# The second attention as one shifted sequence of sixteen two-map units

## The reference

```python
z = h @ w_in;  aq, ak, av, bq, bk, bv = split(z)      # h: 256 tokens; the same for 256 context tokens
bq = rms_norm(bq, qn_g);  bk = rms_norm(bk, kn_g)     # group b: per head of 64
aq, ak, bq, bk = apply_rope_2d(...)                   # latent tokens only
# group a: 4 heads of two maps each, values 128 wide
s = einsum('bqhid,bkhid->bhiqk', q, k) * 64 ** -0.5;  p = softmax(s)
o = einsum('bhqk,bkhe->bqhe', p[:, :, 0] - lam * p[:, :, 1], v)
o = rms_norm(o, subln_g) * (1.0 - lam_init)
# group b: 8 query heads on 2 key/value heads
p = softmax(einsum('bqgrd,bkgd->bgrqk', q, k) * 64 ** -0.5)
o = einsum('bgrqk,bkgd->bqgrd', p, v)
y = concatenate([oa, ob]) @ w_out
x = layer_norm(alpha * x + g1 * y)
x = layer_norm(alpha * x + g2 * mlp(modulate(x, sh2, sc2)))
# mod = silu(c) @ ada_w[l] + ada_b[l] gives shifts, scales and gates, six parts of 1024 a layer
```

## Time and profile before

| | us |
|---|---|
| median of 3 runs | 2010.83 |
| lowest and highest | 1999.68, 2014.06 |
| the profiled execution | 2004.5 |
| its span | 2002.6 |
| end of the last projection before the attention (bv) | 1297.3 |
| start of the scores | 1318.5 |
| start of the output projection | 1419.9 |

### The profile page before, as it was taken

How to read it: one execution, slowest core, us unless ns; L and a number is a source line. 1 busy time by engine, 2 the same in 40 slices (tenths; PEclk the granted TensorE clock), 3 DMA queues, 4 the chain that set the end, 5 groups by cost and what they waited for, 6 DMA issues and landing times.

```text
span 2002.6 us, 38381 instructions
## 1 busy us (share of the span) xinstructions
PE 1820.7 (91%) x13930; PEld 1692.1 (84%) x13930; DVE 1279.4 (64%) x2470; ACT 834.3 (42%) x1510; POOL 112.5 (6%) x101
## 2 busy tenths in 40 slices
PE   6989899999999777899999998967889997889997
PEld 5946899999998545799999998845789997879996
DVE  4455468788744898755655564286666666756665
ACT  4433455455454000255555543322344443434443
POOL 0000000000000454200000000000010001010000
PEclk8979899999999899999999998988999998999999
DMA  6445445555566455355555562310235653525552
GB/s 249 148 147 169 129 156 178 184 177 185 176 180 197 180 209 189 136 179 184 203 180 186 179 227 86 103 44 1 85 116 178 187 182 105 165 97 179 180 187 73
DMA packets 86492, 315.07 MB, mean 157 GB/s; under 512 B 9616, under 2 KB 9760, under 8 KB 86048
## 3 DMA queue, kind: packets, MB, share of 16 engines
q1 hardware_dynamic: 75600, 275.28, 42.6%
q10 hardware_dynamic: 10688, 37.95, 5.3%
q0 software_dynamic: 144, 1.05, 0.1%
HBM read 313.19 MB, written 1.05 MB: 157 GB/s over the span
## 4 chain that ended last, share of the span: by engine, by line
PE 83%; DVE 9%; issue 4%; DMA 1%; ACT 1%; POOL 1%; DVEq 0%; ACTq 0%; POOLq 0%; SPq 0%
PE bank L440 14%; PE bank L441 14%; PE bank L442 14%; PE acc L440 10%; PE acc L441 10%; PE acc L442 10%; PE bank L739 2%; PE bank L522 2%; PE acc L500 2%; DVE route L1599 1%; PE acc L850 1%; POOL route L1264 1%; PE acc L495 1%; DVE arena L1614 1%; DVE small L1704 1%
## 5 line engine op out<-in xcount | busy, mean ns | idle before, releaser
L1304 DVE TENSOR_TENSOR w_lo<-raw,w_hi 128x512 fp32r<-128x512 f32 x982 | 652.8, 689 | 474.6 <-ACT w_hi L934 473.6
L934 ACT ACTIVATE w_hi<-raw 128x512 fp32r<-128x512 f32 x982 | 593.8, 628 | 418.8 <-PE acc L440 268.4
L440 PE MATMUL bank<-x_hi,w_hi 128*128 128x256 f32 x2224 | 639.6, 288 | 53.9 <-issue 22.7
L441 PE MATMUL bank<-x_lo,w_hi 128*128 128x256 f32 x2224 | 636.6, 286 | 0.0
L442 PE MATMUL bank<-x_hi,w_lo 128*128 128x256 f32 x2224 | 636.3, 286 | 0.0
L440 PEld LDWEIGHTS bank<-x_hi,w_hi 128*128 128x128 f32 x2224 | 434.7, 195 | 60.0 <-issue 39.2
L441 PEld LDWEIGHTS bank<-x_lo,w_hi 128*128 128x128 f32 x2224 | 434.7, 195 | 0.0
L442 PEld LDWEIGHTS bank<-x_hi,w_lo 128*128 128x128 f32 x2224 | 434.5, 195 | 0.0
L440 PE MATMUL acc<-x_hi,w_hi 128*128 128x256 f32 x1024 | 290.2, 283 | 0.0
L441 PE MATMUL acc<-x_lo,w_hi 128*128 128x256 f32 x1024 | 289.8, 283 | 0.0
L442 PE MATMUL acc<-x_hi,w_lo 128*128 128x256 f32 x1024 | 289.8, 283 | 0.0
(11 more groups left out here) (231 smaller groups left out, 1891.8 us busy)
## 6 DMA issues: line engine op xcount, KB each, us to landing
raw<-in_peer_u SPq DMA_DIRECT2D x128, 512.0 KB, 3.4
raw<-in_peer_v SPq DMA_DIRECT2D x128, 512.0 KB, 3.3
raw<-in_mlp_w SPq DMA_DIRECT2D x128, 512.0 KB, 3.4
ada_x<-in_ada_w ACTq DMA_DIRECT2D x64, 512.0 KB, 3.9
route<-in_ada_w SPq DMA_DIRECT2D x32, 512.0 KB, 4.4
raw<-in_w_in SPq DMA_DIRECT2D x25, 512.0 KB, 4.1
raw<-in_conv_w_in SPq DMA_DIRECT2D x24, 512.0 KB, 3.9
raw<-in_attn_w_in SPq DMA_DIRECT2D x18, 512.0 KB, 3.4
```

Source lines behind the costliest of these rows:

```text
L440: first = mm(dst, a[0], b[0], start=start, stop=False, **kw)
L441: mm(dst, a[0], b[1], start=False, stop=False, **kw)
L934: return nc.scalar.activation(dst, src, f, **kw)
L1304: v.tensor_tensor(w_lo[:, unit(n, half)], raw[:, a:a + HALF], w_hi[:, unit(n, half)].bitcast(F32), ALU.subtract).then_inc(s["lo_done"], 1)
```

## The change

The rotation is cut in two. Group a's eight tiles are rotated while bq is projected: PE has four matmuls between the two pairs of bq, DVE has its products between the low parts of weight tiles. The mean squares of group b move ahead of the projection of bv. Group b's norm factors and its rotation go into the first steps of the attention, in acc banks.

The diff, cut to its core (`UNITS_2` is 16, `OA` is 13; `attention_order` gives each unit two banks `sc`, then `ams` once behind unit 15, and four `obc` at the end; `t_bank` is acc2 or acc3, `rotate` is the cosine product and the sum of L1737 and L1740):

```diff
                     *softmax_order(MOBA_H, "ms", "mt", 1), ("wo1", 4), ("ms2", 1), ("q", 8), ("s", 8),
-                    ("u", 64), ("route", 2), ("g", 64), ("lam", 1), ("aq", 2), ("ak", 4), ("bq", 2), ("bk", 1),
-                    ("bv", 1), ("bms", 1), ("bbc", 4), ("rot2", 7), *softmax_order(8, "as", "at", 2),
-                    *softmax_order(16, "bs", "bt", 1, {AMS: ("ams", 2)}), ("wo2", 4), ("mean0", 1), ("var0", 1),
+                    ("u", 64), ("route", 2), ("g", 64), ("lam", 1), ("aq", 2), ("ak", 4), ("bq0", 1), ("rot2", 4), ("bq1", 1), ("bk", 1), ("bms", 1),
+                    ("bv", 1), *attention_order(), ("wo2", 4), ("mean0", 1), ("var0", 1),
...
+        sm_pt = cut2(2 * 2 * 512)
+        sm_p = arena[:, 0:2 * 2 * 512]
...
-            ada(ada_at + ADA_RING, 2 * N_MOD * KC)
...
             mlp("mlp0", ins["mlp_w1"][0], ins["mlp_w2"][0])
+            sp.wait_ge(s["ada_row_full"], ADA_1 + ADA_GATES + 1)
+            for n in range(ada_at + ADA_RING, ada_at + 2 * ADA_RING):
+                load_ada(n, slot_free=True)
...
-            project_two("bq", "bq", x_split)
+            project_pair("bq", 0, "bq0", 0, x_split)
+            for k in range(2):
+                wait_freed(pe, "aq", k)
+            for k in range(4):
+                wait_freed(pe, "ak", k)
+            pe.wait_ge(s["in_con2"], 16)
+            mean_heads("rot2", C2("rot"), qk, 8 * T)
+            project_pair("bq", 1, "bq1", 0, x_split)
             project_both("bk", 0, "bk", 0)
...
+            def scores(n):
+                if n < 8:
+                    q, tq, k_tiles = n // 2, n % 2, (14 + n // 2, 4 + n // 2)
+                else:
+                    q, tq, k_tiles = 8 + (n - 8) // 2, n % 2, (13, 12)
+                ps = [opened(f"sc{n}_{m}") for m in range(2)]
+                for k, tile in enumerate(k_tiles):
+                    for m in range(2):
+                        r = slice(64 * m, 64 * m + 64)
+                        last = mm(ps[m][:, k * T:(k + 1) * T], qk[r, q * T + tq * P:q * T + (tq + 1) * P],
+                                  qk[r, tile * T:(tile + 1) * T], start=True, stop=True)
+                        if k:
+                            last.then_inc(full(f"sc{n}_{m}"), 1)
...
+            def transposes(n):
+                pe.wait_ge(s["sm2_p"], n + 1)
+                for b in range(1 if n < 8 else 2):
+                    if n in (0, 1):
+                        pe.wait_ge(s["bbc_done"] if n == 0 else s["rotb_done"], 4 if n == 0 else 3)
+                    elif n < 8:
...
+                    a = (n % 2) * 1024 + b * 512
+                    for m in range(4):
+                        last = nc.tensor.transpose(t_bank(n, b)[:, m * P:(m + 1) * P], sm_p[:, a + m * P:a + (m + 1) * P], C("ident"))
+                    last.then_inc(s["tp_full"], 1)
+            def values(n):
+                pe.wait_ge(s["tp_free"], t_count(n, 0 if n < 8 else 1))
+                tq, a = n % 2, (n % 2) * 1024
...
+                tile_q = (n - 8) // 2
+                o = acc[tile_q // 2][:, (tile_q % 2) * T + tq * P:(tile_q % 2) * T + (tq + 1) * P]
                 for kt in range(4):
+                    for g in range(2):
+                        r = slice(64 * g, 64 * g + 64)
+                        p = sm_pt[:, a + g * 512 + kt * P:a + g * 512 + (kt + 1) * P]
+                        last = mm(o[r, :], bv[:, kt * P + 64 * g:kt * P + 64 * g + 64], p, start=(kt == 0), stop=(kt == 3),
+                                  skip_group_check=True)
...
+            pe.wait_ge(s["a_rope"], 1)
+            for i in range(UNITS_2 + 4):
+                if i == 8:
+                    pe.wait_ge(s["b_rope"], 1)
+                if i < UNITS_2:
+                    scores(i)
+                if i == 0:
+                    pe.wait_ge(s["attn_v_ready"], 4)
+                    pe.wait_ge(s["b_rstd"], 1)
...
+                if i == 2:
+                    pe.wait_ge(s["bbc_done"], 4)
+                    for k, n in enumerate((2 * T, 2 * T, T)):
+                        a = 8 * T + 2 * k * T
+                        mm(acc[(0, 1, 3)[k]][:, 0:n], C2("rot"), qk[:, a:a + n], start=True, stop=True).then_inc(s["rotb_full"], 1)
...
+                if 3 <= i < UNITS_2 + 3:
+                    transposes(i - 3)
+                if i >= 4:
+                    if i == 4:
+                        pe.wait_ge(s["rotb_done"], 2)
+                    if i == 12:
+                        wait_freed(pe, "bv")
+                        pe.wait_ge(s["oa_copied"], 2)
+                    last = values(i - 4)
+                    if i - 4 == 7:
+                        last.then_inc(s["attn_oa_full"], 1)
+                if i == OA + 5:
+                    pe.wait_ge(s["oa_mask"], 1)
+                    for g in range(4):
+                        mm(opened("obc", g)[:, 0:T], norm_row("one", g), oa_mask[32 * g:32 * g + 32, :], start=True, stop=True)\
+                            .then_inc(full("obc", g), 1)
...
                 mean(f"mean{n}", res3d, lambda k: wait_res(pe, n, k))
                 mean(f"var{n}", res_sq3d, lambda k: pe.wait_ge(s["ln_sq"], 4 * n + k + 1))
+                if n < ADA_2:
+                    ada(ADA_1 + ADA_GATES + n, acc[0], acc[1], first=True)
+                    ada_columns(ADA_1 + ADA_GATES + n, acc[1])
...
             def mlp(n):
+                pe.wait_ge(s["ada_cols_ready"], ADA_1 + ADA_GATES + n + 1)
                 zero_acc()
...
+            def copies(n):
+                for b in range(1 if n < 8 else 2):
+                    act.wait_ge(s["tp_full"], t_count(n, b))
+                    a = (n % 2) * 1024 + b * 512
+                    fn(sm_pt[:, a:a + 512], t_bank(n, b)[:, :], ACT.Copy).then_inc(s["tp_free"], 1)
+            for i in range(1, UNITS_2 + 4):
+                if i >= 4:
+                    copies(i - 4)
+                if i <= UNITS_2:
+                    exps(i - 1)
+                if i == OA + 1:
                     act.wait_ge(s["oa_ready"], 1)
                     fn(oa_sq, oa_sq, ACT.Square).then_inc(s["oa_sq"], 1)
+                if i == UNITS_2:
+                    wait_full(act, "ams")
+                    fn(oa_std, B("ams")[:, 0:T], ACT.Sqrt, scale=2.0 ** -10, bias=C("eps_small")).then_inc(free("ams"), 1)
+            x_high("mixed2", mixed2, x_hi, 0)
...
+            for k in range(4):
+                wait_full(dve, "rot2", k)
+                turn(qk_rot[:, k * 512:(k + 1) * 512], B("rot2", k)[:, :], 2).then_inc(free("rot2", k), 1)
+                if k % 2:
+                    lo_next("bq", 2 + k // 2)
+            for k in range(4):
+                wait_freed(dve, "rot2", k)
+            step(rotate(0, 4))
+            lo_next("bk", 0)
+            rotate(4, 4).then_inc(s["a_rope"], 1)
+            for name in ("av", "bv"):
                 for q in range(TILE[name][1]):
                     lo_next(name, q)
...
+            def oa_factor():
+                wait_freed(dve, "ams")
+                then_wait(v.reciprocal(oa_mask, oa_std))
                 finite = float(np.sqrt(FMAX / P) / 32.0)
+                v.scalar_tensor_tensor(oa_mask, oa_std, finite, oa_mask, ALU.is_lt, ALU.mult).then_inc(s["oa_mask"], 1)
             def oa_norm():
+                for g in range(4):
+                    a = slice(g * T, (g + 1) * T)
+                    wait_full(dve, "obc", g)
+                    v.scalar_tensor_tensor(mixed2[:, a], B("obc", g)[:, 0:T], lamw[:, 5:6], oa[:, a], ALU.mult, ALU.mult)\
+                        .then_inc(free("obc", g), 1)
+            b_norm(0)
+            b_norm(1)
+            for i in range(1, UNITS_2 + 3):
+                if i == 12:
+                    oa_copy()
+                if i == 13:
+                    oa_clamp()
+                if i <= UNITS_2:
+                    maxima(i - 1)
+                if i == 1:
+                    b_norm(2)
+                    b_norm(3)
+                if 2 <= i <= UNITS_2 + 1:
+                    probabilities(i - 2)
+                if i == 3:
+                    b_turn(0)
+                    b_turn(1)
+                if i == 4:
+                    b_turn(2)
+                    for k in range(3):
+                        dve.wait_ge(s["rotb_done"], k + 1)
+                    rotate(8, 5).then_inc(s["b_rope"], 1)
+                if i == UNITS_2 + 1:
+                    oa_factor()
+            oa_norm()
+            x_low("mixed2", mixed2, x_hi, x_lo, 0)
...
+                if n < ADA_2:
+                    adaln(ADA_1 + ADA_GATES + n, acc[1])
```

More of the change, by code:

```diff
@@ L798, in _ @@
             project_rows("av", [acc[n][:, :] for n in range(4)], tokens, s["attn_v_full"])
+            pe.wait_ge(s["b_sq"], 1)
+            ps = opened("bms")
+            for c in range(6):
+                g = c % 4
+                last = mm(ps[32 * g:32 * g + 32, 0:T], head_means(c // 4), qk_sq[:, c * T:(c + 1) * T], start=(c < 4),
+                          stop=(c >= 2), skip_group_check=True)
```

(15 more changed lines are left out.)

288 lines of the change are left out of this document (107 added, 181 removed).

## The result

The changed kernel took **1952.82 us** (median, 1947.37 to 1955.28), the kernel before beside it 2006.53: ratio 0.9728, 95% interval 0.9682 to 0.9773. So it is faster by 54 us; 42.6 were forecast. The profiled executions took 2004.5 and 1947.37 us, 57 apart.

| stretch | before, us | after, us | difference |
|---|---|---|---|
| start to the first product of aq (code that was not changed) | 1204.72 | 1198.86 | -5.9 |
| from there to the second half of the first `w_out2` tile | 218.98 | 168.76 | -50.2 |
| from there to the end | 578.9 | 578.0 | -0.9 |

A forecast was written before the change was run, and what follows sets the result against it. PE, busy 91% of the span, was taken as the bound. Terms 4.3 + 33.1 + 30.4 + 4 + 7.0 = 78.8 against 126.4, plus 4 clock and 1 norms, gave 42.6 us less: 1968 us, range 1948 to 1988.

The forecast's parts named there:

- the ring through DVE's copy: Group b before: PE's transposes, DVE's copy, PE's products and scores, DVE's maxima form a closed ring, one unit per 3.72 us.
- In front: Ahead of the attention units: four rotation matmuls and the mean squares, moved among the projections, cost PE 4.3 us.
- The cover that I named: Projections of bq, bk and av hide DVE's rotation work of 7.2 us, costed at nothing; uncovered, up to 7.2.
- Group a: First eight attention units, bound by DVE at 2.99 us each, with norm, rotation and other DVE work: 33.1 us.
- Group b and joints: PE's remaining work in group b, 30.4 us with two-head value products at 1.3, plus 4 us for joints between stretches.
- Hand-over: From the last value product to the second half of the output projection's first tile: 7.0 us, 3.2 worse than before.
- Clock: Stops at the start of the unit sequence put PE at the lower level for 8 us, a loss of 4.
- Layer norms: Modulation rounds moved into norms 0 and 1 cost +1 us for both, ends -2 and +5.
- the better end: Rival, chance 0.12: value products fully side by side, no clock fall, norm 0 gets 2 us back: 1959 us.
- The clock's case: Rival, chance 0.10: PE runs at 1.2 GHz through half of the attention sequence: 1984 us.
- projections in the way: Rival, chance 0.10: rotation delays DVE's low parts, PE stands in bq, bk or av up to 7.2 us: 1975.
- the ring: Rival, chance 0.03: the attention ring closes again with one unit in flight, 7.8 us a unit: 2030 us.

The follow-up runs named there:

- run 1: Kernel before, with ScalarE instead of VectorE copying the transposed probabilities out of PSUM: 1992.01 us, ratio to before 0.9936.
- run 2: Changed kernel with the rotation of group a's q and k put back behind the last projection: 1960.68 us.
- run 6: Changed kernel with group b's norm and rotation moved from units 0 to 4 to between the scores of units 7 and 8: 1956.86 us.
- run 3: Changed kernel with the copies of the transposed probabilities put back on VectorE: 1957.85 us.
- run 4: Changed kernel with the value products of a two-head unit of group b issued head after head, not by turns: 1952.61 us.
- run 5: Changed kernel with the scores of a unit issued map after map, not by turns: 1952.03 us.
- run 7: Changed kernel with the two passes that end group b's rotation moved from VectorE to GpSimd: 1953.26 us.
- run 8: Changed kernel with group a's norm broadcasts ahead of the last transposes and group b's output split straight from PSUM: 1942.36 us, ratio to before 0.9696.
- run 9: Changed kernel run again without any edit: 1948.66 us, ratio to before 0.9709.
- run 10: Changed kernel with products of zeros on TensorE as fillers in five of its longest waits: 1948.64 us.
- run 12: Changed kernel with run 8's edit and run 10's fillers except those ahead of w_out2, second execution of that version: 1936.62 us, ratio to before 0.9654.

## Why the prediction was right, and where its sizes were off

The mechanism held: the ring through DVE's copy is shown by run 1, group a bound by DVE and group b by PE by the windows and the timelines. Where the stage's 50.2 us are from: rotation beside the projections 9.3 (run 2), norm beside group a 6.1 (run 6). Run 1 had neither, nor two-head units, and its stage was 205.71, 36.95 above the changed kernel's. Without those two 21.5 are left: two-head units 8 x (5.32 - 3.11) = 17.7, worked out and not run alone, and 3.8 for joints and the rest. With the copy's 13.3 that makes 50.2. In the 3.8 are things that no run moved alone: the modulation rounds, whose matmuls were 4.44 us (L500) and 2.01 us (L495) of PE's busy time inside the stage before, the packed norm, the two groups in one sequence, and against them a hand-over 3.0 us longer (6.8 for 3.8). And the shares depend on the order in which one takes the parts out: the copy is 13.3 in the kernel before (run 1) and 8.2 in the changed one (run 3), and 3.4 of the 9.3 came with the lower level.

Term by term, forecast and measured:

- **In front**: 4.3, and 4.7 (the last projection's work ended 97.30 us from aq, and 92.61 before). The cover that I named held, with no wait of PE inside the projections of bq, bk, av and bv; run 2 shows what it was worth, 5.9 of the 7.2.
- **Group a**: 33.1, and 34.3. DVE as forecast at 3.01 us a unit; until scores and first factors existed it took 2.2 us and not 1.4, and the rest is in small parts.
- **Group b and joints**: 30.4 + 4, and 30.4 together: 26.6 of work and 3.7 of stops (1.24, 0.40, 0.68, 1.37). The work was mis-sized: the value product for two heads was taken at 1.3 us and is 1.02 (-2.2 over eight), and four transposes were taken at 0.6 and are 0.51 when issued in eights (-1.5 over seventeen). For the first the Trainium skill's page "TensorEngine Tiling (Array Packing)", section "Theoretical Speedup", had the better number: its "up to 2x" for 64 columns is what the row shows, 16 records in 1.09 us where one head had 8, as long as the heads take turns; head after head it was 1.51 (run 4). My 1.3 took the share of a 32-column product over to a shape that doesn't lose it.
- **Hand-over**: 7.0, and 6.8.
- **Clock**: 4, and nothing that I can find in the stage. From 1304 to 1320 PE had 0.65, 1.00, 0.71 and 0.87 in four windows of 4 us, some 6 us at the lower level by these shares, where 8 were forecast; but DVE's row is full there, and PE's slower work lies under it. In the changed kernel and in runs 4, 5, 7, 8 and 9 the scores of unit 2 took from 1.38 to 1.92 us, by the level, and the wait at unit 1's transposes ended 9.8 us after they began in every one of them. This is the step that failed most: I priced PE's lost clock where PE wasn't the bound. Runs 2 and 10, with more of the ramp at 0.50, show from where on it costs: in run 10 the wait at unit 1's transposes came 11.2 us after unit 2's scores instead of 9.8, so 1.4 us.
- **Layer norms**: +1, and -0.9 to the end of the kernel. Norm 0's gap is filled: the zeroing ran partly at the lower level, 5.40 us, the MLP began 0.3 us later behind the mean than before, but at 1.00 and not at 0.55, and the stretch from mean 0 to mean 1 got 1.2 shorter. The rows that answer to the earlier trace rows:

```profile
1404.88 5.40 PE L767 MATMUL acc<-con 128*128 128x512 f32 x8 [1.28 <-DVE small L1392]
1409.71 0.68 PE L457 MATMUL bank<-x_hi,w_hi 128*128 128x256 f32 x1
```

- **Not in the sum**: 5.9 us in code that wasn't changed, ahead of the stage. 2.3 of it were there by 272 us, in the first block; the other 3.6 came in the stretch of the retrieval layer. That stretch, 650 to 850 us, ran at 0.93 before and 0.95 after, and in the other executions at 0.90 to 0.96, and its length follows the level: between the same two low parts (at 634.9 and 856.2 us before) it was 4.6 us shorter than before at 0.96 (run 8) and 5.6 and 6.0 longer at 0.90 (runs 2 and 12). That the level there isn't the same twice is measured; why, isn't. The forecast had no term for it, so for the forecast these 5.9 are luck.

In the stage 82.8 us were forecast (with the clock) and 76.2 measured, 6.6 less; 1.9 in the norms and the 5.9 ahead make 14.4, against 57.1 - 42.6 = 14.5 between the profiled executions. Between the medians, 54 - 42.6, it was 11.

The rivals: the better end came (1953 for its 1959), with its side-by-side value products and norm 0; its third condition, no fall of the clock, did not hold, the fall just cost nothing; and the 6 us from 1959 to 1953 are about the size of the luck named above. The clock's case did not come, nor projections in the way, nor the ring.

## What to carry to other kernels

Where two engines pass a tile around, look for the closed ring first and take one member's work out of it: moving one copy gave 13 us of 2000, and pairing heads, by the unit times, an estimated 18 more. Price the lower clock only where PE decides, and a pass moved "beside" other work only by the engine that decides there. Look at the hand-over behind a sequence as well: here splitting the result straight from PSUM, with the broadcasts earlier, gave 5.7 us, the kept clock included. And a stretch that nobody changed can differ by 10 us between executions, so compare inside a stage, counted from its own start.

## What the hardware showed that I had not expected

- Eight value products of two heads, on two 64-column halves of the array: 1.02 us by turns, 1.51 head after head, 1.02 for one head alone. Scores on two 64-row halves: 1.07 in either order.
- While GpSimd ran an SBUF pass of 2.9 us, VectorE's operations on a few SBUF elements took up to 2.87 us instead of 0.16, and two reductions from PSUM their usual 1.28.
- The clock level over the same code differs from execution to execution (0.90 to 0.96 over 650 to 850 us), and aq started anywhere from 1195.89 to 1206.63 us, 10.7 apart.
- A lower level under a full VectorE row cost nothing: the scores of unit 2 took from 1.38 to 1.92 us, and what followed came at the same time, 9.8 us after they began. In run 10, where they took 2.08, it came 11.2 us after.
